# A hybrid decoder step: a stacked tail for the heads' states, norm sums by VectorE at later steps, and the convolution norm's squares in halves

## The reference

```python
# convolution branch: layer norm over 1024 features
mu = jnp.mean(cf, -1, keepdims=True)
var = jnp.mean(jnp.square(cf - mu), -1, keepdims=True)
cn = (cf - mu) * lax.rsqrt(var + EPS) * conv_ln_g + conv_ln_b
y_a = jax.nn.silu(cn) @ w_conv_out
# retention branch, per head (DK 256, DV 512): outputs, new state, norm over DV
o = scores @ v + q_dec @ S
S_new = exp(L * lg) * S + einsum('bjhd,bjhe->bhde', k_dec, v)
omu = jnp.mean(o, -1, keepdims=True)
ovar = jnp.mean(jnp.square(o - omu), -1, keepdims=True)
on = (o - omu) * lax.rsqrt(ovar + EPS) * ret_gn_g
```

## Time and profile before

| | |
|---|---|
| median of 3 runs | 805.98 us (805.79 to 806.58) |
| the profiled execution, its own time | 805.64 us |
| its span from first to last instruction | 803.7 us |
| mean granted TensorE clock | 0.987 of full |
| TensorE busy | 774.3 us (96%) |
| VectorE busy | 664.9 us (83%) |
| ScalarE busy | 508.4 us (63%) |
| data moved by DMA | 213.27 MB, 265 GB/s on the mean |

### The profile page before, as it was taken

How to read it: one execution, slowest core, us unless ns; L and a number is a source line. 1 busy time by engine, 2 the same in 40 slices (tenths; PEclk the granted TensorE clock), 3 DMA queues, 4 the chain that set the end, 5 groups by cost and what they waited for, 6 DMA issues and landing times.

```text
span 803.7 us, 12108 instructions
## 1 busy us (share of the span) xinstructions
PE 774.3 (96%) x4755; PEld 659.7 (82%) x4755; DVE 664.9 (83%) x891; ACT 508.4 (63%) x632; POOL 96.9 (12%) x120
## 2 busy tenths in 40 slices
PE   8989999999999999999699899999999999999994
PEld 5989999767676689999699894888888888888873
DVE  5698999767677879899867567988998899899987
ACT  7434446475767676345476363788888888888863
POOL 0100000233243200000002001011111211110000
PEclk9999999999999999999989999999999999999998
DMA  8945454689887836445348544799999999999972
GB/s 338 388 154 179 165 192 154 237 310 319 296 294 263 312 131 211 146 177 177 138 153 306 210 175 159 288 348 380 375 377 359 371 358 360 365 365 370 349 282 81
DMA packets 39173, 213.27 MB, mean 265 GB/s; under 512 B 7381, under 2 KB 7637, under 8 KB 19244
## 3 DMA queue, kind: packets, MB, share of 16 engines
q1 hardware_dynamic: 23268, 165.39, 55.3%
q0 software_dynamic: 15408, 45.71, 16.3%
q10 hardware_dynamic: 432, 1.31, 0.4%
HBM read 193.45 MB, written 31.65 MB: 280 GB/s over the span
## 4 chain that ended last, share of the span: by engine, by line
PE 86%; DVE 9%; ACT 3%; issue 1%; DMA 1%; DVEq 0%; ACTq 0%
PE bank L1580 35%; PE bank L1854 33%; PE bank L1692 3%; PE bank L1727 2%; DVE w_lo L1089 2%; PE bank L1638 2%; DVE conv L1136 2%; PE bank L1844 2%; PE bank L1742 1%; PE bank L1756 1%; PE bank L1763 1%; PE bank L1703 1%; ACT w_hi L755 1%; PE bank L1884 1%; PE bank L1606 1%
## 5 line engine op out<-in xcount | busy, mean ns | idle before, releaser
L1580 PE MATMUL bank<-h_hi,w_hi 128*128 128x264 f32 (+1 forms) x640 | 189.4, 296 | 3.4 <-DVE w_lo L1089 3.4
L1580 PE MATMUL bank<-h_lo,w_hi 128*128 128x264 f32 (+1 forms) x640 | 184.7, 289 | 0.0
L1580 PE MATMUL bank<-h_hi,w_lo 128*128 128x264 f32 (+1 forms) x640 | 184.6, 288 | 0.0
L1094 DVE TENSOR_TENSOR ring_lo<-raw,ring_hi 128x2048 fp32r<-128x2048 f32 x72 | 163.6, 2289 | 23.4 <-ACT ring_hi L762 23.4
L1089 DVE TENSOR_TENSOR w_lo<-raw,w_hi 128x1024 fp32r<-128x1024 f32 x112 | 136.8, 1221 | 38.7 <-ACT w_hi L755 38.4
L755 ACT ACTIVATE w_hi<-raw 128x1024 fp32r<-128x1024 f32 x112 | 117.9, 1052 | 69.7 <-PE bank L1580 69.4
L762 ACT ACTIVATE ring_hi<-raw 128x2048 fp32r<-128x2048 f32 x72 | 138.2, 1920 | 19.7 <-PE bank L1854 19.7
L1580 PEld LDWEIGHTS bank<-h_hi,w_hi 128*128 128x128 f32 x640 | 121.2, 189 | 8.8 <-DVE w_lo L1089 5.4
L1580 PEld LDWEIGHTS bank<-h_lo,w_hi 128*128 128x128 f32 x640 | 121.2, 189 | 0.6 <-issue 0.2
L1580 PEld LDWEIGHTS bank<-h_hi,w_lo 128*128 128x128 f32 x640 | 121.0, 189 | 0.0
L1136 DVE SCALAR_TENSOR_TENSOR conv<-u,vec,conv 128x256 f32<-128x256 f32 x240 | 101.6, 477 | 0.2
(11 more groups left out here) (283 smaller groups left out, 1492.7 us busy)
## 6 DMA issues: line engine op xcount, KB each, us to landing
raw<-weights SPq DMA_DIRECT2D x152, 1024.0 KB, 7.3
S_ring<-in_state_ret POOLq DMA_DIRECT2D x26, 512.0 KB, 6.6
out_ret_sample<-S_ring POOLq DMA_DIRECT2D x26, 512.0 KB, 6.5
S_five<-in_state_ret POOLq DMA_DIRECT2D x6, 512.0 KB, 4.9
out_ret_sample<-S_five POOLq DMA_DIRECT2D x6, 512.0 KB, 7.5
out_ret_prompt<-S_out POOLq DMA_DIRECT2D x8, 256.0 KB, 4.7
y_rows<-xg POOLq DMA_DIRECT2D x4, 512.0 KB, 5.7
raw<-y_rows SPq DMA_DIRECT2D x2, 1024.0 KB, 6.0
```

The lines of the kernel that those rows point to most:

```text
L1094: dve.tensor_tensor(ring_view(ring_lo, k), raw[raw_slot(NCM + k)][:, :].rearrange("p (k n) -> p k n", k=4), ring_view(ring_hi, k).bitcast( ...
L1580: ins = pe.matmul(out, a[:, k, cols], b[:, k0 + k, :], start=first and k == 0 and j == 0, stop=last and k == ks - 1 and j == 2)
```

## The change

It has three parts.

1. The tail of a head's state. The 16 last tokens' k are held as `k_two`: their high part in rows 0 to 15 and again in rows 32 to 47, the low part in rows 64 to 79; `v_two` gets 24 rows more, with a high part of v in rows 64 to 79. One product of 80 rows in the replicated type (f32r) takes the place of an f32 product of 16 rows, twice a head. ScalarE makes one copy more per head of each of `k_two` and `v_two`, VectorE the low part of `k_two` (behind the update of step k % 4 == 0), which also frees the bank.
2. The norm of heads 0 to 2. VectorE adds the four blocks of a head (`halved`) for the mean at steps 6, 10, 14 and for the squares at steps 8, 12, 16. TensorE makes one product of each. The means move from steps 6, 10, 14 to 7, 11, 15, the variances from 7, 11, 15 to 9, 13, 17; head 3 stays at 18 and 19 with four products each.
3. The convolution norm. The subtraction and the squares are made in halves of four blocks; the squares stand at unit 88 behind the split instead of at 87; the variance's product and root stand at unit 90 (before 89), the activations begin at 91 (before 90).

```diff
-LN_SUM, LN_MEAN, LN_VAR, LN_SIG, LN_OUT = (FIRST["cout"] - n for n in (11, 9, 7, 6, 5))
+LN_SUM, LN_MEAN, LN_VAR, LN_SIG, LN_OUT = (FIRST["cout"] - n for n in (11, 9, 6, 5, 5))
 QUOTA = [(LN_SUM + 1, 0), (FIRST["ret"], 4), (STEP0 + 15, 1), (STEP0, 4), (FIRST["v"], 4), (FIRST["q"], 2), (4, 3), (0, 0)]
+GM_AT, GV_AT, GM_SUM, GV_SUM = (7, 11, 15, 18), (9, 13, 17, 19), (6, 10, 14), (8, 12, 16)
...
-                add((("kt", k // 4, 1), "A"))
+                add((("kt", k // 4, 1), "K"))
...
             for w in range(NMIX):
                 s, i = UNITS[w]
                 hi(w + 2)
+                if w == LN_MEAN + 1:
+                    all_stored(act)
+                    for hf in range(2):
+                        act.wait_ge(cdev_ready, hf + 1)
+                        act.activation(ln_sq[:, 4 * hf:4 * hf + 4, OUT], conv[:, 4 * hf:4 * hf + 4, OUT], ACT.Square).then_inc(csq_ready, 1)
 
...
                         h = k // 4
-                        for tt in range(3):
-                            nt = min(128, TP - TOKENS[tt][0])
-                            nm = ("kt", h, 0 if tt < 2 else 1)
-                            seen(act, nm)
-                            col = tt * DK if tt < 2 else 0
-                            ins = act.activation(k_tok[0:nt, tt, :], bank(nm)[0:nt, col:col + DK], ACT.Copy,
-                                                 scale=kdecay[0:nt, tt, h:h + 1])
-                            if tt:
-                                free(ins)
+                        for tt in range(2):
+                            seen(act, ("kt", h, 0))
+                            ins = act.activation(k_tok[:, tt, :], bank(("kt", h, 0))[:, tt * DK:tt * DK + DK], ACT.Copy,
+                                                 scale=kdecay[:, tt, h:h + 1])
+                        free(ins)
+                        seen(act, ("kt", h, 1))
+                        for q in (32, 0):
+                            act.activation(k_two[q:q + 16, :], bank(("kt", h, 1))[0:16, 0:DK], ACT.Copy,
+                                           scale=kdecay[0:16, 2, h:h + 1]).then_inc(khi_ready, 1)
                     if k < 16 and k % 4 == 1:
                         h = k // 4
...
                         act.wait_ge(vlo_ready, h - 1)
+                        seen(act, ("S", h - 2, 1))
+                    act.activation(v_two[64:80, h % 2, :], v_tok[h][0:16, 2, :], ACT.Copy).then_inc(vhi_ready, 1)
                     act.activation(v_two[0:24, h % 2, :], v_tok[h][0:24, 2, :], ACT.Copy).then_inc(vhi_ready, 1)
...
-                if w == LN_MEAN:
-                    evacuated(act, ("lm",))
-                    all_stored(act)
-                    act.activation(ln_sq[:, :, OUT], conv[:, :, OUT], ACT.Square).then_inc(csq_ready, 1)
...
-            def halved(src):
-
-                n = KT
+            def halved(dst, src, n):
+
                 while n > 1:
                     n //= 2
-                    ins = dve.tensor_tensor(ln_sq[:, 0:n, OUT], src[:, 0:n, OUT], src[:, n:2 * n, OUT], ALU.add)
-                    src = ln_sq
+                    ins = dve.tensor_tensor(dst[:, 0:n, OUT], src[:, 0:n, OUT], src[:, n:2 * n, OUT], ALU.add)
+                    src = dst
                     if n > 1:
                         link(ins)
-                ins.then_inc(csum_ready, 1)
+                return ins
...
+                    dve.memset(k_two[:, :].bitcast(f32), 0.0).then_inc(two_clear, 1)
...
+                    if k < 16 and k % 4 == 0:
+                        h = k // 4
+                        dve.wait_ge(khi_ready, 2 * h + 2)
+                        dve.scalar_tensor_tensor(out=k_two[64:80, :], in0=bank(("kt", h, 1))[0:16, 0:DK], scalar=kdecay[0:16, 2, h:h + 1],
+                                                 in1=k_two[0:16, :].bitcast(f32), op0=ALU.mult, op1=ALU.subtract).then_inc(klo_ready, 1)
...
+                    if k in GM_SUM:
+                        h = GM_SUM.index(k)
+                        evacuated(dve, ("ot", h))
+                        halved(gsq, oT[:, 4 * h:4 * h + 4, :], 4).then_inc(gsum_ready, 1)
+                    if k in GV_SUM:
+                        dve.wait_ge(osq_ready, GV_SUM.index(k) + 1)
+                        halved(gsq, gsq, 4).then_inc(gsum_ready, 1)
...
-                    halved(conv)
+                    halved(ln_sq, conv, KT).then_inc(csum_ready, 1)
                 if w == LN_MEAN:
                     seen(dve, ("lm",))
-                    mb = bank(("lm",))[:, OUT].rearrange("p (a t) -> p a t", a=1).broadcast_to([128, KT, N])
-                    free(dve.tensor_tensor(conv[:, :, OUT], conv[:, :, OUT], mb, ALU.subtract))
-                if w == LN_VAR - 1:
-                    dve.wait_ge(csq_ready, 1)
-                    halved(ln_sq)
+                    mb = bank(("lm",))[:, OUT].rearrange("p (a t) -> p a t", a=1).broadcast_to([128, 4, N])
+                    for hf in range(2):
+                        dve.tensor_tensor(conv[:, 4 * hf:4 * hf + 4, OUT], conv[:, 4 * hf:4 * hf + 4, OUT], mb, ALU.subtract).then_inc(cdev_ready, 1)
+                    dve.wait_ge(cdev_ready, 2)
+                    free(dve.nop())
+                if w == LN_MEAN + 1:
+                    dve.wait_ge(csq_ready, 2)
+                    halved(ln_sq, ln_sq, KT).then_inc(csum_ready, 1)
...
+                        evacuated(pe, ("kt", h, 0))
                         evacuated(pe, ("kt", h, 1))
+                        pe.wait_ge(vlo_ready, h + 1)
                         for dt in range(2):
                             b = opened(("S", h, dt))
-                            for tt, nt in enumerate((128, 128, 16)):
-                                ins = pe.matmul(b[:, :], k_tok[0:nt, tt, dt * 128:(dt + 1) * 128],
-                                                v_tok[h][0:nt, tt, :], start=tt == 0, stop=tt == 2)
-                            done(ins)
+                            for tt in range(2):
+                                pe.matmul(b[:, :], k_tok[:, tt, dt * 128:(dt + 1) * 128], v_tok[h][:, tt, :], start=tt == 0, stop=False)
+                            done(pe.matmul(b[:, :], k_two[:, dt * 128:(dt + 1) * 128], v_two[:, h % 2, :], start=False, stop=True))
...
-                    if k >= 6 and (k - 6) % 4 == 0 and k <= 18:
-                        h = (k - 6) // 4
-                        evacuated(pe, ("ot", h))
-                        b = opened(("gm", h))
-                        for et in range(4):
-                            ins = pe.matmul(b[:, OUT], cst("mean_v"), oT[:, 4 * h + et, OUT], start=et == 0, stop=et == 3)
-                        done(ins)
-                    if k >= 7 and (k - 7) % 4 == 0 and k <= 19:
-                        h = (k - 7) // 4
-                        pe.wait_ge(osq_ready, h + 1)
-                        b = opened(("gv", h))
-                        for et in range(4):
-                            ins = pe.matmul(b[:, OUT], cst("mean_v"), gsq[:, et, OUT], start=et == 0, stop=et == 3)
-                        done(ins)
+                    if k in GM_AT:
+                        h = GM_AT.index(k)
+                        if h < NH - 1:
+                            pe.wait_ge(gsum_ready, 2 * h + 1)
+                            b = opened(("gm", h))
+                            done(pe.matmul(b[:, OUT], cst("mean_v"), gsq[:, 0, OUT], start=True, stop=True))
+                        else:
+                            evacuated(pe, ("ot", h))
+                            b = opened(("gm", h))
+                            for et in range(4):
+                                ins = pe.matmul(b[:, OUT], cst("mean_v"), oT[:, 4 * h + et, OUT], start=et == 0, stop=et == 3)
+                            done(ins)
```

54 lines of the change are left out of this document (33 added, 21 removed).

## The result

The changed kernel took 811.8 us (median of 14 runs, 809.37 to 814.87), the kernel before in the same rounds 807.01 us (14 runs, 805.68 to 809.26): ratio 1.0057, 95% interval 1.0044 to 1.0069. I had forecast 800.5 us, faster. The profiled execution is the longest of the fourteen, 814.87 us; its parts are read beside those of before with that in mind.

The account below looks back on a forecast made before the run. TensorE, 96% busy, looked like the bound, but in the retention VectorE and ScalarE would make it wait. Gains of 1.2 (retention) and 4.3 us (convolution norm) off 805.64 gave 800.1, plus 0.34 for the median: 800.5 us; range 793.5 to 804.5.

Parts of the forecast that it names:

- What is taken from TensorE: Retention: TensorE loses 14.3 us of work, 5.4 in the state products and 8.9 in the norm sums.
- two terms of the state product: Retention, state tail: each 16-row product taken as 0.955 us, its 80-row replacement as 0.28; 5.4 us saved.
- Why the saving isn't kept: Retention: TensorE waits for VectorE and ScalarE, so the last variance product starts only 1.2 us earlier.
- waits to step 12: Retention: TensorE waits 0.6, 1.9, 1.4 and 1.5 us at steps 4, 8, 10 and 12, sum 5.4.
- steps 14, 17 and 19: End of the retention: TensorE waits 2.9 us, about 1.6 for osb, and 2.7 for the last Square.
- The chain from the broadcast of step 13 to the last variance product: Retention: VectorE and ScalarE set the time from 254.05 to 293.6 us, 1.2 us earlier at the end.
- the charge for the clock: Convolution norm: nothing charged for lower clock behind waits of 1.4 and 3.1 us, though up to 2.3 might go.
- The convolution norm: Convolution product starts at 419.6 us against 423.91, gain 4.3 us, bounds 2.0 and 5.0.
- That TensorE stays the bound: Rival, retention: TensorE's 14.3 us are kept, 787.4 us; or met half way, 789 to 796; together chance 0.25.
- That the norm's gain is eaten by late rounds: Rival, convolution norm: ScalarE's rounds begin no sooner, only 1.2 us gained, 804.8 us; chance 0.10.
- The ring of slots: Rival, retention: five state slots decide, loads land 3 us later per head, 6.5 us slower, 812.5 us; chance 0.08.

Follow-up runs that it names:

- `e5_tail_and_sums`: Changed kernel without part 3 (parts 1 and 2 together, the convolution norm as before): 812.76 us, ratio 1.0057 against the kernel before.
- The filled kernel: Changed kernel plus redundant products, results overwritten, in TensorE's waits at steps 4, 8, 12, the last variance and the convolution product: 804.74 us, ratio 0.9961 against before.
- late squares: Changed kernel with ScalarE's squares of heads 0 to 2 a unit later, behind the next unit's split: 804.07 us, ratio 0.9962 against before.
- the tail alone: Kernel before plus part 1 only, norm sums and convolution norm as before: 802.31 us, ratio 0.9945 against before.
- two heads with and without filling: Changed kernel with late squares, head 2's sums left with TensorE: 801.57 us; with redundant products at step 4, convolution product and output product: 795.33 us.
- tail and convolution norm filled: Kernel before plus parts 1 and 3, with redundant products at step 4 and ahead of the convolution and output products: 796.43 us, ratio 0.9863 against before.
- the best kernel: Changed kernel with late squares, head 2's sums left with TensorE, redundant products in three places: 795.33 us, ratio 0.9835 against before.

## Why the prediction was wrong, point by point

**What is taken from TensorE: right for the norm, two terms of the state product mis-sized.** The six norm products are a quarter each, as forecast. For the state product I took 5.4 us; its two halves now start 1.96 us apart, and the whole takes 3.92 us a head (203.63 to 207.55) in place of 5.83: 7.6 us. Both terms of the difference were too small. Two f32 products of 128 rows and then the new one start at

```profile
203.63 1.88 PE L1713 MATMUL bank<-v,k_tok 128*128 128x512 f32 x4
204.96 0.80 PE L1714 MATMUL bank<-v_two,k_two 80*128 80x512 f32 x1
205.59 1.88 PE L1713 MATMUL bank<-v,k_tok 128*128 128x512 f32 x4
```

so the two take 1.33 us, 0.66 each, and the new one 0.63 where I took 0.28. A group of three took 2.92 us before; less those 1.33 that is 1.6 us for the product of 16 rows, by this estimate, where I took the group's mean of 0.955. The errors cancel but for 0.3 us a product. The weight loads show where the 1.6 us lie, in before

```profile
203.37 0.19 PEld L1692 LDWEIGHTS bank<-v,k_tok 128*128 128x128 f32 x1 [0.24 <-issue]
204.32 0.29 PEld L1692 LDWEIGHTS bank<-v,k_tok 16*128 16x128 f32 x2 [0.76 <-issue]
205.37 0.30 PEld L1692 LDWEIGHTS bank<-v,k_tok 128*128 128x128 f32 x2 [0.76 <-issue]
```

and after

```profile
204.50 0.19 PEld L1713 LDWEIGHTS bank<-v,k_tok 128*128 128x128 f32 x1 [0.24 <-issue]
204.93 0.19 PEld L1714 LDWEIGHTS bank<-v_two,k_two 80*128 80x128 f32 x1 [0.24 <-issue]
205.36 0.43 PEld L1713 LDWEIGHTS bank<-v,k_tok 128*128 128x128 f32 x2 [0.24 <-issue]
```

Going to 16 rows and back leaves gaps of 0.76 us where loads of like height leave 0.24.

**Why the saving isn't kept: right in mechanism, waits to step 12 somewhat too small.** I had 0.6, 1.9, 1.4 and 1.5 us at steps 4, 8, 10 and 12; they were 2.3 (a second wait at the unit behind), 2.6, 0.5 and 2.3, in all 2.3 us more. (At step 8 my own terms add up to 208.6 and not 208.3, which makes that wait 2.2.) For steps 14, 17 and 19 I had 2.9, 1.6 and 2.7 us; they were 1.9, 1.65 and 2.61. The chain from the broadcast of step 13 to the last variance product I gave 39.55 us; it took 39.50 (262.84 to 302.34), closer than its pieces: the three waits in it sum to 6.15 us for 7.2.

**The step that failed: the charge for the clock.** The prediction says of the convolution norm "I charge nothing, since both waits are shorter than that one", and it makes no charge at all in the retention. Five of the waits that it forecast itself, at steps 4, 8, 12, 19 and at the convolution product, had a slow unit behind them, 1.5 us each, 7.5 us in all in the profiled execution (in the trace of `e5_tail_and_sums` the last variance has none, so this is the upper end). The filled kernel gives 7 us back, and such products in two waits of the kernel before gain 2.3. With 7.5 us for clock and 2.3 for waits the forecast would have been 810.3, beside 811.8, or 808.6 once the 1.7 us are taken off that three state products saved beyond my term up to step 13. The 3 us that are left aren't assigned: the two stretches that the change doesn't touch cost 4.6 us in the profiled execution, and their share in the median isn't known. I had a row of such a slow unit before my eyes and read it as if only a wait so long did it; it was the longest wait of that stage, not the shortest that costs clock.

**The convolution norm: the number right, its working not.** 4.3 us were forecast from the norm to the convolution product and 4.3 came (9.35 us late at the mean, 5.07 at the product), with waits of 1.60 and 2.65 us for the 1.4 and 3.1 forecast. But the last terms as I wrote them, 407.5, three rounds of 2.94 "less one of them without activations" and 0.8, make at most 417.1 and not 419.6, so that the start came out to 0.1 us is not to the credit of that sum. Only 1.9 us of it reach the time alone, through the slow unit and the stretch ahead of the experts.

**The rivals.** That TensorE stays the bound was wrong: it did wait. That the norm's gain is eaten by late rounds was wrong as well. The ring of slots gave the nearest time (812.5) by another mechanism: a state landing late is one link of the chain at step 8, but ScalarE's waits for states sum to 17.3 us before, 25.8 in the changed kernel and 30.6 with late squares, which is 7.7 us faster, and filling, which loads no state sooner, brings the loss back. The true rival, that short waits let the clock fall, was not on my list with a chance of its own.

**What stays open.** The stretch from the tables of the experts to their first product took 15.6 to 15.7 us in the profiled executions of five kernels (before, the tail alone, two heads with and without filling, tail and convolution norm filled) and 17.2 to 18.5 us in the others. Its windows, before and after:

```profile
487.57:503.23 15.66, 14.86 (x58) 8.66 (x58) 11.59 (x40) 5.45 (x9) 3.43 (x3) 0.89 0.27 92
```

```profile
494.22:512.61 18.39, 18.20 (x57) 10.33 (x57) 11.67 (x40) 5.44 (x9) 3.25 (x3) 0.72 0.23 79
```

The clock is lower for longer, with the same work. What in the time ahead of it decides was not tried. Nor was the changed kernel with its state loads earlier.

## What to carry to other kernels

A wait of TensorE can cost more than its length: price each forecast wait of some 2 us or more with the unit behind it at the lower clock (1.5 us here; the table below shows how often), and compare that with what is saved. Where such a wait can't be shortened, cheap redundant products in it are worth their place; where it can, look for the one line of dependent pieces on the other engines and move what isn't due yet behind the piece that is. Two edits that shorten the same engine's steps need not add up (here 4.4 us faster and 2.6 slower made 4.6 slower); time them together.

## What the runs showed of the hardware

- The main waits in the 14 traces, and how often the unit behind them ran at a granted clock of 0.50 to 0.70 and took 4.3 to 5.4 us in place of 3.0 to 3.2:

| place | wait, us | slow unit behind it |
|---|---|---|
| early unit, the same code in all | 2.6 | 7 of 14 |
| step 4, two waits | 1.9 to 2.3 in all | 5 of 5 |
| step 4, two waits (the tail alone) | 1.2 in all | 0 of 1 |
| step 8 | 1.9, 2.6 | 2 of 2 |
| step 8, two waits | 1.6, 1.7 in all | 0 of 1, 1 of 1 |
| step 12 | 2.3 | 2 of 2 |
| steps 14 and 17, split of unit 93 | 1.6 | 0 of 18 |
| last variance | 2.6 | 2 of 4 |
| mean of the convolution norm, two waits | 1.8 in all | 4 of 14 |
| variance of the convolution norm | 3.1 to 4.6 | 4 of 4 |
| convolution product | 2.6 | 5 of 5 |
| output product | 2.9 | 10 of 10 |

- So length alone doesn't decide: the same code behind the same wait does both (the early unit took 3.2 us in before and 4.7 after, 49.80 to 53.00 and 50.17 to 54.89), and what else decides isn't shown. That this makes the spread of the times (805.7 to 809.3 before, 792.5 to 799.1 in the best kernel) would fit and wasn't tested.
- An f32 product of 16 rows between two of 128 took some 1.6 us, by the difference above, where one of 128 rows takes 0.66: 5.83 us for two groups of three, 3.92 with the 16 rows as part of an 80-row f32r product.
